# A two-layer encoder in one kernel: cross attention, norm and routing ordered by token tile, and roots on GpSimd

## The reference

```
h = h + cross_attention(rms_norm(h, ln_cross), rms_norm(mem, ln_mem), wq, wkv, wo)   # 4 heads of 128
h = h + hier_moe(rms_norm(h, ln_ffn), ...)
# cross: softmax(q k^T / sqrt(128)) v per head, heads concatenated, times wo
# hier_moe: group logits (4) and expert logits (4 x 4) from the normed token;
#   best group, its two best experts, weights = softmax over the two, times the group's probability;
#   y = sum of gate * (silu(t Wg) * (t Wu)) Wd, 16 experts of 1024 x 512
return rms_norm(h, ln_final)
```

## Time and profile before

| what | value |
|---|---|
| runs, median (lowest to highest) | 977.0 us (976.87 to 977.29) |
| profiled execution, its own time | 976.23 us |
| its span | 974.6 us |
| mean granted TensorE clock | 0.992 |
| PE busy | 945.1 us, 97% |
| DVE, ACT, POOL busy | 395.2, 196.4, 11.1 us |
| read from HBM | 280.76 MB, 289 GB/s over the span |

### The profile page before, as it was taken

The page is one execution under the profiler, slowest core; times in us unless marked ns, Lnnn a source line. Parts: engine busy times, 40 slices in busy tenths (PEclk is TensorE's granted clock), DMA queues, the critical chain, the costliest instruction groups (busy, mean ns, idle before and its releaser), DMA issues.

```text
span 974.6 us, 12424 instructions
## 1 busy us (share of the span) xinstructions
PE 945.1 (97%) x4968; PEld 587.4 (60%) x4968; DVE 395.2 (41%) x860; ACT 196.4 (20%) x392; POOL 11.1 (1%) x21
## 2 busy tenths in 40 slices
PE   8999999999999999999999999999999998999995
PEld 5568558563333333388999999999575433333332
DVE  4325423342121212167766676665544411212115
ACT  3005402133212221221011011100132231212102
POOL 1110000000000000000000000000000000000000
PEclk9999999999999999999999999999999899999998
DMA  9894285359999999999875557653694699999993
GB/s 342 293 352 147 87 363 197 139 196 390 383 428 430 426 428 421 392 281 251 188 200 145 149 151 185 170 181 126 295 406 176 203 378 430 429 428 424 421 416 151
DMA packets 116278, 282.53 MB, mean 290 GB/s; under 512 B 4726, under 2 KB 82886, under 8 KB 104200
## 3 DMA queue, kind: packets, MB, share of 16 engines
q1 hardware_dynamic: 114784, 278.18, 77.5%
q0 software_dynamic: 1168, 3.40, 1.0%
q10 hardware_dynamic: 280, 0.31, 0.1%
HBM read 280.76 MB, written 1.11 MB: 289 GB/s over the span
## 4 chain that ended last, share of the span: by engine, by line
PE 88%; DMA 8%; DVE 2%; ACT 1%; issue 1%; SPq 0%; DVEq 0%
PE banks L1311 82%; DMA ring<-expert_w_up_in 7%; PE banks L1314 4%; PE banks L1706 2%; DMA ring<-xkv_w_in 1%; ACT late L853 0%; DVE scratch L2592 0%; ACT nrm L1053 0%; DVE mx L2301 0%; DVE nrm L2243 0%; DVE nrm L2309 0%; DVE scratch L2504 0%; DVE tmp L2095 0%; DVE late L846 0%; DVE late L2343 0%
## 5 line engine op out<-in xcount | busy, mean ns | idle before, releaser
L1311 PE MATMUL banks<-ring,scratch 128*64 128x512 f32 (+2 forms) x1696 | 422.5, 568 | 8.2 <-DMA ring<-expert_w_up_in 7.4
L1311 PEld LDWEIGHTS banks<-ring,scratch 128*64 128x64 f32 (+1 forms) x1696 | 159.9, 147 | 213.4 <-issue 212.7
L1311 PE MATMUL banks<-late,ring 128*128 128x256 f32 (+1 forms) x704 | 119.6, 330 | 0.8 <-ACT late L853 0.7
L1311 PEld LDWEIGHTS banks<-late,ring 128*128 128x128 f32 x704 | 107.4, 191 | 11.0 <-issue 1.6
L1008 ACT ACTIVATE scratch<-banks 128x512 f32<-128x512 f32 (+4 forms) x84 | 57.9, 701 | 272.5 <-PE banks L1314 186.0
L1311 PE MATMUL banks<-scratch 128*128 128x128 f32 (+5 forms) x492 | 110.5, 390 | 1.5 <-DVE scratch L2592 1.5
L2586 DVE TENSOR_SCALAR scratch<-banks 32x1024 f32<-32x1024 f32 x28 | 34.2, 1223 | 191.0 <-PE banks L1311 190.8
L1311 PEld LDWEIGHTS banks<-scratch 128*128 128x128 f32 (+2 forms) x492 | 60.8, 173 | 44.6 <-issue 38.5
L1311 PE MATMUL banks<-ring,late 128*128 128x512 f32 (+3 forms) x288 | 82.8, 442 | 1.0 <-DVE late L2343 1.0
L1311 PE MATMUL banks<-scratch,ring 128*128 128x128 f32 (+1 forms) x464 | 70.0, 308 | 0.8 <-DMA ring<-xkv_w_in 0.8
L1311 PEld LDWEIGHTS banks<-ring,late 128*128 128x128 f32 x288 | 49.2, 190 | 30.8 <-issue 24.9
(11 more groups left out here) (213 smaller groups left out, 677.9 us busy)
## 6 DMA issues: line engine op xcount, KB each, us to landing
ring<-expert_w_gate_in SPq DMA_DIRECT2D x22, 2048.0 KB, 15.4
ring<-expert_w_down_in SPq DMA_DIRECT2D x22, 2048.0 KB, 13.3
ring<-expert_w_up_in SPq DMA_DIRECT2D x20, 2048.0 KB, 16.0
ring<-odd_w_in_in SPq DMA_DIRECT2D x72, 512.0 KB, 6.5
ring<-expert_w_down_in SPq DMA_DIRECT2D x24, 512.0 KB, 10.9
ring<-xkv_w_in SPq DMA_DIRECT2D x4, 2048.0 KB, 11.9
scratch<-expert_w_gate_in SPq DMA_DIRECT2D x4, 2048.0 KB, 9.9
ring<-expert_w_up_in SPq DMA_DIRECT2D x16, 512.0 KB, 8.3
```

Of the source, the lines that this page charges most:

```text
L1311: return giving_back(nc.tensor.matmul(dst, lhsT, rhs, start=start, stop=stop))
```

## The change

Norms "3" and "6" no longer go through the shared norm. The raw rows of h are flipped in five groups (`TURNS`: tile, chunks, bank) and copied out as they are ready; the router's logits, the ranks, the mask, the positions, the first selectors and the first gathers are made for each tile by itself. Tile 0's flips and router products stand between tile 1's projection products. `keep_busy` is gone; in layer 0 the values of layer 1 are cut into pieces between the router's and positions' products. In layer 1's cross attention the last query block, and products of the first output tile (head by head), stand between the heads' steps; the piece `xq1b` is copied by DVE instead of ACT (`xq1a` by ACT). DVE makes the gates after the first gathers are copied. The roots of norms "2" to "7" are made by POOL: one `tensor_scalar` for the mean and one `tensor_tensor` with `ALU.pow` and an exponent of -0.5; the sums of squares carry the factor 1/1024 already. SP issues the late slot's first half when the projection is done. The new groups of chunks and gathers have banks and semaphores of their own. The core of the diff:

```diff
         E_BANK = (6, 7, 0, 1)
+        X_BANK = (0, 1, 2, 3), (6, 7, 2, 3)
+        TURNS = ((0, range(0, 4), 4), (0, range(4, 8), 0), (1, range(0, 4), 1), (1, range(4, 6), 4), (1, range(6, 8), 0))
+        TURNED_BY_ACT = (1, 2, 4)
+        TURNED_BY_DVE = (0, 3)
+        ROUTER_BANK = (5, 2)
+        FAR_BANK = {2: 3, 3: 1}
...
-                        piece_in(sp, f"router{l}")
+                        sp.wait_ge(proj, (R_X0 if l == 0 else R_X1 - 4) + 4)
...
+        BY_POOL = "234567"
...
+                if name in "36":
+                    l = "36".index(name)
+                    copy_turned(act, True, l, 1)
+                    act.wait_ge(root0_set, l + 1)
+                    rows_for_gathers(0)
+                    copy_turned(act, True, l, 2)
+                    copy_turned(act, True, l, 4)
+                    act.wait_ge(rstd_set, i + 1)
+                    rows_for_gathers(1)
+                    return
...
-                exps(a + 2)
-                pT_out(a + 1)
-                exps(a + 3)
+                if l:
+                    queries_out(1)
+                    pT_out(a)
+                    pT_out(a + 1)
+                    exps(a + 2)
+                    exps(a + 3)
+                else:
+                    pT_out(a)
+                    exps(a + 2)
+                    pT_out(a + 1)
+                    exps(a + 3)
...
+            def root_of_means(name):
+                i = NORM_SEQ[name]
+                sums, rst = ssq[:, i], roots[:, i]
+                n = BY_POOL.index(name)
+                squares = sum(1 if before in "47" else 2 for before in BY_POOL[:n + 1])
+
+                def mean(t, *parts):
+                    return nc.gpsimd.tensor_scalar(var[:, t:t + 1], sums[:, parts[0]:parts[0] + 1], EPS,
+                                                   sums[:, parts[1]:parts[1] + 1] if parts[1:] else None, ALU.add,
+                                                   *([ALU.add] if parts[1:] else []))
+
+                def root_of(tiles):
+                    return nc.gpsimd.tensor_tensor(rst[:, tiles], var[:, tiles], half_power[:, tiles], ALU.pow)
+
+                def added():
+                    means[0] += 1
+                    pool.wait_ge(sums_set, means[0])
+
+                pool.wait_ge(ssq_act, i + 1)
+                if name in "36":
+                    mean(0, 0).then_inc(sums_set, 1)
+                    added()
+                    root_of(slice(0, 1)).then_inc(root0_set, 1)
+                    pool.wait_ge(ssq_dve, squares)
+                    mean(1, 1, 2).then_inc(sums_set, 1)
+                    added()
+                    root_of(slice(1, 2)).then_inc(rstd_set, 1)
+                    return
+                if name in "47":
+                    mean(0, 0, 2)
+                else:
+                    mean(0, 0)
+                pool.wait_ge(ssq_dve, squares)
+                mean(1, 1, 3 if name in "47" else 2).then_inc(sums_set, 1)
+                added()
...
+                def out_part(t, f, heads):
+                    for j in heads:
+                        if t == 0 and f == 0:
+                            pe.wait_ge(pv_sb, A_X[l] + j + 1)
+                        w = slot(W_XO[l]).rearrange("p (j n) -> p j n", j=4)
+                        last = mm(bank[X_BANK[l][2 * t + f]][:, :], cross_yT[:, j, t * P:(t + 1) * P],
+                                  w[:, j, f * 512:(f + 1) * 512], j == 0, j == X_HEADS - 1)
+                    if j == X_HEADS - 1:
+                        last.then_inc(proj, 1)
+
...
+                    out_part(0, 0, range(4))
+                    out_part(0, 1, range(4))
+                else:
+                    second_queries((0,))
+                    head_scores(0)
+                    head_scores(1)
+                    second_queries((1,))
+                    transposes(a)
+                    transposes(a + 1)
+                    head_scores(2)
+                    head_scores(3)
+                    head_outputs(0)
+                    head_outputs(1)
+                    arrived(pe, W_XO[l])
+                    out_part(0, 0, (0,))
+                    transposes(a + 2)
+                    out_part(0, 1, (0,))
+                    transposes(a + 3)
+                    out_part(0, 0, (1,))
+                    head_outputs(2)
+                    out_part(0, 1, (1,))
+                    head_outputs(3)
+                    out_part(0, 0, (2,))
+                    out_part(0, 1, (2,))
+                    out_part(0, 0, (3,))
+                    out_part(0, 1, (3,))
+
+                out_part(1, 0, range(4))
+                turn(l, 0)
+                turn(l, 1)
+                out_part(1, 1, range(2))
+                router(l, 0, range(CH))
+                turn(l, 2)
+                out_part(1, 1, range(2, 4))
+                slots_read()
...
+            def turn(l, n):
+
+                t, chunks, b = TURNS[n]
+                pe.wait_ge(resid, (R_X0, R_X1)[l] + 2 + (t and 1 + chunks[0] // 4))
+                for i, c in enumerate(chunks):
+                    last = flip(bank[b][:, i * P:(i + 1) * P], h[:, t, c * P:(c + 1) * P])
+                last.then_inc(turned, 1)
...
+            def router(l, t, chunks):
+
+                for c in chunks:
+                    if c == 0 and t == 0:
+                        pe.wait_ge(router_in, ROUTER)
+                    for n, group in enumerate(TURNS):
+                        if group[0] == t and group[1][0] == c:
+                            turned_out(pe, l, n)
+                    last = mm(bank[ROUTER_BANK[t]][:, t * NR:(t + 1) * NR], xg[:, c, t, :], rw[:, l, c, :], c == 0, c == CH - 1)
...
+                def positions(t):
+                    pe.wait_ge(mask_set, TILES * l + t + 1)
+                    b = bank[ROUTER_BANK[t]]
+                    chosen = mask[:, t].rearrange("p g e -> p (g e)")
+                    for n, counted in enumerate((earlier, ones)):
+                        at = POSITIONS + n * EXPERTS
+                        last = mm(b[:, at:at + EXPERTS], counted, chosen, True, True)
+                    last.then_inc(pos_ps, 1)
+
+                def first_gathers(t, order):
+                    pe.wait_ge(first_sel, TILES * l + t + 1)
+                    pe.wait_ge(nrm_set, TILES * l + t + 1)
+                    for j in order:
+                        if t == 0 and j < 2:
+                            piece_free(pe, f"gather{l}0{j}")
+                        for i in range(2):
+                            at = i * SEQ + t * P
+                            last = mm(first_gather(l, j)[:, at:at + P], nrm[:, t, 2 * j + i, :], sel[:, 0, t], True, True)
...
+
+                router(l, 1, range(4))
+                turn(l, 3)
...
-
-                if l == 0:
-                    values(1, 1)
+                    value_part(0, range(3))
+                    positions(0)
+                    router(l, 1, range(4, CH))
+                    value_part(0, range(3, CH))
+                    positions(1)
+                    value_part(1, range(CH))
                     slots_read()
+                    for t in range(TILES):
+                        first_gathers(t, (0, 2, 1, 3))
                 else:
-                    keep_busy(2)
-
-                pe.wait_ge(mask_set, l + 1)
-                b = bank[5]
-                both = mask.rearrange("p t g e -> p (t g e)")
-                mm(b[:, 0:TILES * EXPERTS], earlier, both, True, True)
-                mm(b[:, TILES * EXPERTS:2 * TILES * EXPERTS], ones, both, True, True).then_inc(pos_ps, 1)
-                if l:
-                    keep_busy(1)
+                    positions(0)
+                    router(l, 1, range(4, CH))
+                    first_gathers(0, range(4))
+                    positions(1)
+                    first_gathers(1, range(4))
 
                 def gather(g, j):
...
+                    elif name in "36":
+                        l = "36".index(name)
+                        for j in range(3):
+                            add(at, j)
+                        copy_turned(dve, False, l, 0)
+                        dve.wait_ge(resid, at + 3)
+                        squares(0)
+                        dve.wait_ge(root0_set, l + 1)
+                        choose(l, 0)
+                        add(at, 3)
+                        dve.wait_ge(resid, at + 4)
+                        squares(1)
+                        copy_turned(dve, False, l, 3)
+                        place(l, 0)
                     else:
                         add(at, 0)
...
+            def choose(l, t):
+
+                dve.wait_ge(router_in, ROUTER)
+                dve.wait_ge(router_ps, TILES * l + t + 1)
+                step(v.scalar_tensor_tensor(out=lg[:, t], in0=bank[ROUTER_BANK[t]][:, t * NR:(t + 1) * NR],
...
-                step(v.tensor_reduce(rank, above.rearrange("p (n j) -> p n j", j=EPG - 1), AX.X, ALU.add))
```

(22 more changed lines are left out.)

373 lines of the change are left out of this document (211 added, 162 removed).

## The result

The median of the changed kernel's four runs is 962.64 us (960.93 to 964.21) beside 977.14 us of four runs of the kernel before: a ratio of 0.9843 (95% interval 0.9822 to 0.9864). The profiled execution took 964.07 us (span 962.5) beside 976.23 (span 974.6), a difference of 12.2 us.

A forecast was written before the change was run, and what follows sets the result against it. TensorE, busy for 97% of the span, was taken to bound the kernel. Gains of 6.9 + 2.4 + 1.1 = 10.4 us took the profiled 976.23 to 965.8; with the median 0.8 higher the forecast was 966.6, range 963.5 to 972.5.

The forecast's parts named there:

- Layer 0: Layer 0, projection to first gate product: 37.7 us of work instead of 39.97, a gain of 2.8 us, 2.4 after DMA.
- the charge for DMA: Layer 0's expert loads: a backlog of up to 1.6 us, mostly taken by slack, charged at 0.4 us.
- The last root: Final norm: GpSimd's sum and power take 1.5 us instead of VectorE's 2.6, a gain of 1.1 us at the end.
- the size of layer 1: Layer 1: first gate product at 758.3 instead of 765.21, a gain of 6.9 us, 2.9 in cross attention and 4.0 behind.
- Cross attention: Layer 1: query and output products cover the softmax waits; first output tile complete at 738.7 instead of 741.65, gain 2.9 us.
- From the complete first tile to the first gate product: Layer 1, projection of tile 1, routing and gathers by tile: from 738.7 to 758.3, a gain of 4.0 us.
- (a): Rival: without fillers the clock falls in layer 1's routing and stays down into the gate products, costing 3.3 us: 969.9; chance 0.22.
- (b): Rival: DMA eats the expert stages' gain; layer 0's shift returns as a stall, layer 1 loses 1 us: 969.4; chance 0.13.
- (c): Rival: GpSimd's sum and power take 4 us, losing 2.5 at the end and 2.4 in layer 1: 971.5; chance 0.15.
- (d): Rival: GpSimd's root chain so long that the kernel is slower than before, 981 at 8 us a chain; chance 0.04.
- (e): Rival: gaps between tiles; hand-offs eat half of layer 1's routing gain and 1 us of layer 0: 969.6; chance 0.12.
- a wait for the second tile's selectors: Sign in the profile after: TensorE waiting for these selectors, or for a root, was to mean (c) or (e).

The follow-up runs named there:

- before_no_filler: The kernel before without its three products on the identity in layer 1: 979.83 us, ratio to before 1.0013.
- late_half_late: The changed kernel with the late half of an expert matrix sent when the router is done, not at the projection's end: 965.58 us, ratio 0.9862.
- filler_in_stall: The changed kernel with two identity products ahead of the third expert pair's up products, where TensorE waits for weights: 963.02 us, ratio 0.9857.

## Why the prediction was wrong by 4 us and right in its mechanism

**Right.** Direction and order of the gains (layer 1, layer 0, end); no identity products, output products between turned probabilities, and a gate product that moves by what TensorE's queue loses, with the stalls moving along. Layer 0: forecast 2.8 before the charge for DMA, measured 3.09; the stretch from the projection was 37.56 us for 37.7, and the start on head 0 gave 0.68 instead of 0.52. The last root: a chain of 1.5 us forecast, 1.37 measured; 1.1 forecast, 1.34 gained.

**The step that failed** is the size of layer 1: 6.9 us forecast, 9.00 measured with the clock up, as forecast. The slow router of the profile of before is in both numbers, since I had taken its rows. Most of the 2.1 us is one error, made in both parts: I laid group after group with the duration of the row, though the next group starts before that duration is over, and rounded up. The rest, 0.65 us, is a wait that I had put into the path and that is not there.
- Cross attention: 2.9 forecast for the first tile's completion, 3.63 measured (33.22 to 29.59 us behind the query products). The half query piece was right to 0.2 us (until 724.0 by before's clock, forecast 724.2). Then I placed the first product with the output weights at 729.0, and it came at 728.55 by the same clock. Two heads' scores are 1.89 us in the row and 1.73 from start to start (716.80 to 718.53); over four such groups of two that is 0.55 us (one of them took 1.83), and the rounding is the rest.
- From the complete first tile to the first gate product: 19.6 us forecast, 18.19 measured. Of the 1.4 us, 0.4 are the projection with its insertions (10.3 against 9.92), 0.4 the last turns and the second router half (3.5 against 3.12), and 0.65 the end. Tile 1's positions, selectors and gathers were to take 4.0 us, because I let VectorE count for the capacity flag only when the first chunk was gathered, so that its scaling ended 0.7 us behind the gathers. In the trace the counts stand beside the start of the gathers (752.04 to 752.99), the scaling begins at 753.10, its first two chunks are done at 753.96, and the gate product stands directly behind the gathers at 754.15, 3.3 us after tile 0's:

```profile
753.10 1.65 DVE L2742 TENSOR_SCALAR scratch<-banks,gains 128x256 f32<-128x256 f32 x4
```


**Two smaller ones.** I charged 0.4 us for a DMA backlog behind layer 0; the middle shows 0.14 in this pair and −0.14 to +0.14 over the five profiles of the changed kernel. And I had taken the runs' median as 0.8 us above the profiled execution on both sides; the single execution moves by up to 2.6 us at the start and by 1.5 us in layer 1, whichever kernel it is. At the start the profile of before stood at 147.63 and that of after at 148.52, where all profiles lie between 145.94 and 149.14. So of the 4.0 us between forecast and median 2.6 are the terms above (13.0 us in the pair for 10.4), and the rest is which executions the two medians fell on: the median of the changed kernel's 12 runs is 963.9, and in the executions of the two kernels with a mean granted clock of 0.992 the medians stand 12.1 us apart (976.2 of six, 964.1 of two). The four-run median is the one that lies outside the range; that of the 12 runs lies inside it. But two of the five profiles lost 1.5 us in layer 1 to a clock fall that the forecast did not hold, so a hit by that median would be luck in part, since the terms fell short by 2.6 us.

**The rivals.** (a) The clock falls: true in some executions, at 1.5 us instead of 3.3, since it came back before the gate products. Its premise, that the fillers had brought the clock back in the kernel before, is not borne out: in before_no_filler it came back without them. The Trainium skill (TensorE: Matmul & The Clock Gate, What's actually happening) has the throttled state as the default that activity lifts; by that rule removing the fillers is a risk, and the five profiles of the changed kernel fit it in two cases and not in three; in the kernel before, the fillers were worth 0.2 us in the one pair of profiles that there is. (b) DMA: refuted by the middle column and late_half_late, and the fall behind the stall by filler_in_stall. (c), (d) The power: 0.57 us for one column and 0.72 for two, not several us. The slope that I gave them was right at the end, where 2.3 us more cost 2.30, and in layer 1 right only beyond a slack of 0.7 us, where 1.9 us more cost 1.18. (e) Hand-offs: they cost less than drawn. Two of my signs were badly put: a wait for the second tile's selectors stands there (0.69 us) without (c) or (e), since my own drawing held one, and GpSimd's instructions at the end took 0.81, 0.29 and 0.72 us, not under 0.6 each.
By the Trainium skill (GPSIMD Engine Reference, Performance versus the Vector engine) elementwise work runs at half VectorE's speed on GpSimd. For the small instruction that makes the mean the rows give 0.22 to 0.30 us on GpSimd (one column, at the end 0.81 once) and 0.15 to 0.17 on VectorE (one or two columns), so the trace agrees roughly; the move pays because one power replaces seven dependent steps (a seed and three iterations of two).

## What to carry to other kernels

When one tile's dependent small steps can stand beside the other tile's products, the gain can be nearly all of the idle time; lay out such a queue by start-to-start distances, not by the durations of the rows, which reach into the next row. Before pricing a clock fall, take several profiles of the same kernel: here one program lost between nothing and 2.6 us at its start and 1.5 us or nothing in layer 1. Before reading a gain off a pair of profiles, compare the rows that nobody edited: one router took 4.87 or 3.87 us. And ask of each stage what sets its pace: a slow stretch in front of transfers that are late anyway costs nothing.

## What the runs showed that I had not expected

- One TensorE queue, two clocks: the 16 records of 128 columns of tile 0's first gathers took 2.03 us in three profiles of the changed kernel and 3.5 to 3.6 in two, with the same instructions ahead of them. What was different is not known.
- GpSimd's power has no long first call here: the first one (two columns, at 140.66) took 0.73 us, the later ones 0.72.
- GpSimd's instruction for the mean took 0.22 to 0.30 us everywhere but at the end. There the first took 0.81 us and ended at 955.81, 0.08 us behind the end of VectorE's squares (955.03 to 955.73), beside which it ran; the second took 0.29 us. The cause was not tested. It was on the chain, at little cost: the second started 0.15 us behind the read-out of the squares, where it is 0.10 in the other norms, so about 0.05 us.
